# Closing stage of a decoder step: the gate's gain moved behind the transpose, idle products ahead, tile order 64-128-128, last tile stored in halves

## The reference, cut to what matters

```python
h = h + hier_moe(hn, ...)
gate = jax.nn.sigmoid(rmsnorm(h, g_ple) @ w_ple_gate)
h = h + (p @ w_ple) * gate
y = rmsnorm(h, g_final)
```

## Time and profile before

| | |
|---|---|
| time of the kernel, median of 3 | 748.12 us (746.76 to 748.71) |
| the profiled execution: its time, and its span from first to last instruction | 748.71 us, 748.7 us |
| TensorE busy | 701.7 us (94%) |
| VectorE, ScalarE, GpSimd busy | 504.4, 443.5, 143.7 us |
| mean granted clock of TensorE | 0.947 of full speed |
| HBM traffic | 322 GB/s over the span |

### The profile page before, as it was taken

The page is one execution under the profiler, slowest core; times in us unless marked ns, Lnnn a source line. Parts: engine busy times, 40 slices in busy tenths (PEclk is TensorE's granted clock), DMA queues, the critical chain, the costliest instruction groups (busy, mean ns, idle before and its releaser), DMA issues.

```text
span 748.7 us, 9169 instructions
## 1 busy us (share of the span) xinstructions
PE 701.7 (94%) x2912; PEld 470.0 (63%) x2912; DVE 504.4 (67%) x585; ACT 443.5 (59%) x436; POOL 143.7 (19%) x168
## 2 busy tenths in 40 slices
PE   2999999799999999999999999999999999994894
PEld 2646644458667777777777777777767677772441
DVE  5164013654878779787797877978779587963544
ACT  3012101344878777787777877778777777860245
POOL 4000000123302313123131221303313021311000
PEclk9899789787999999999999999999999899997797
DMA  9973031617999999999999999999999999794202
GB/s 281 371 299 113 22 113 47 249 40 313 326 423 398 426 410 408 413 400 423 398 402 427 400 415 409 402 402 395 425 408 379 402 362 428 309 346 160 55 0 70
DMA packets 30202, 233.40 MB, mean 312 GB/s; under 512 B 8023, under 2 KB 9367, under 8 KB 17375
## 3 DMA queue, kind: packets, MB, share of 16 engines
q1 hardware_dynamic: 22221, 226.96, 76.2%
q0 software_dynamic: 4480, 5.26, 2.2%
q10 hardware_dynamic: 3482, 0.94, 0.6%
HBM read 231.67 MB, written 9.32 MB: 322 GB/s over the span
## 4 chain that ended last, share of the span: by engine, by line
PE 83%; DMA 8%; DVE 5%; ACT 2%; issue 1%; POOL 1%; POOLq 0%; SPq 0%; DVEq 0%; ACTq 0%
PE ps L763 20%; PE ps L760 16%; PE ps L761 16%; PE ps L775 7%; DMA ring<-in_w_eg_dram 6%; PE ps L670 5%; PE ps L832 5%; PE ps L584 3%; PE ps L564 2%; PE ps L609 2%; PE ps L623 2%; PE ps L709 2%; PE ps L732 1%; DVE perm L1039 1%; DMA xg<-hn_rows,cur 1%
## 5 line engine op out<-in xcount | busy, mean ns | idle before, releaser
L1266 DVE TENSOR_TENSOR lo<-ring,hi 128x1536 fp32r<-128x1536 f32 x192 | 333.2, 1753 | 68.4 <-PE ps L763 51.6
L929 ACT ACTIVATE hi<-ring 128x1536 fp32r<-128x1536 f32 x192 | 280.9, 1485 | 88.8 <-PE ps L763 72.9
L760 PE MATMUL ps<-hi,xr 128*128 128x512 f32 x384 | 194.2, 506 | 0.0
L761 PE MATMUL ps<-lo,xr 128*128 128x512 f32 x384 | 152.8, 398 | 0.0
L763 PE MATMUL ps<-ring,xz 128*128 128x512 f32 x256 | 131.9, 597 | 0.0
L760 PE MATMUL ps<-hi,hr 128*128 128x512 f32 x192 | 96.2, 501 | 1.6 <-DVE hr L1278 1.6
L760 PEld LDWEIGHTS ps<-hi,xr 128*128 128x128 f32 x384 | 73.5, 191 | 36.1 <-issue 21.0
L761 PEld LDWEIGHTS ps<-lo,xr 128*128 128x128 f32 x384 | 73.4, 191 | 34.9 <-issue 23.3
L514 POOL DMA_INDIRECT moe_rows<-yo,cur x32 | 49.9, 1560 | 197.0 <-DVE yo L1256 197.0
L938 ACT ACTIVATE gu<-ps 128x512 f32<-128x512 f32 x64 | 69.3, 1082 | 30.8 <-PE ps L763 30.8
L761 PE MATMUL ps<-lo,hr 128*128 128x512 f32 x192 | 75.9, 395 | 0.0
(11 more groups left out here) (195 smaller groups left out, 591.3 us busy)
## 6 DMA issues: line engine op xcount, KB each, us to landing
ring<-in_w_eg_dram SPq DMA_DIRECT2D x32, 2048.0 KB, 14.6
ring<-in_w_eu_dram SPq DMA_DIRECT2D x32, 2048.0 KB, 15.5
ring<-in_w_ed_dram SPq DMA_DIRECT2D x31, 2048.0 KB, 16.5
ring<-in_w_in_dram SPq DMA_DIRECT2D x3, 2048.0 KB, 15.2
ring<-in_w_out_dram SPq DMA_DIRECT2D x2, 2048.0 KB, 22.3
ring<-in_w_ple_gate_dram SPq DMA_DIRECT2D x2, 2048.0 KB, 8.1
ring<-in_w_ed_dram SPq DMA_DIRECT2D x2, 1024.0 KB, 7.5
ring<-moe_rows SPq DMA_DIRECT2D x4, 512.0 KB, 5.5
```

The source lines that it names most:

```text
L760: mm(out, parts, hi[:, u % HI_RING, cut], start=begin, stop=False)
L761: done = mm(out, parts, lo[:, u % LO_RING, cut], start=False, stop=end)
L929: acti(hi[:, u % HI_RING, :], ring[:, u // 2, off:off + SPLIT], ACT.Copy).then_inc(hi_ready, counted(u, first, last))
L1266: V.tensor_tensor(lo[:, u % LO_RING, :], ring[:, u // 2, off:off + SPLIT], hi[:, u % HI_RING, :].bitcast(F32), ALU.subtract).then_inc(lo_r ...
```

## The change

The gain `g_ple` is no longer broadcast and multiplied into the rows. It is loaded once, at the start, as one value for each partition and block (`g_cols`, on ScalarE's queue), TensorE turns the rows of `h` themselves, and the copy out of PSUM multiplies by `g_cols`. Ahead of this stand 12 idle products that wait for nothing. The tiles go in the order 2, 0, 1. The adds of a tile are spread between the copies of the tile before. The last tile (tile 1) is finished and stored in two halves. The diff, cut to its core:

```diff
+LAST_ORDER = (2, 0, 1)
+        g_cols = sb("g_cols", [P, KC])
+        sig = (mixT_flat[:, 0:D], win_flat[:, 0:D], mixT_flat[:, D:2 * D])
@@ sync
-            for c, g in enumerate((g_ple, g_final.rearrange("(o d) -> o d", o=1))):
-                sp.dma_start(ring[:, 5, c * D:(c + 1) * D], g.partition_broadcast(P).rearrange(
-                    "q o d -> q (o d)")).then_inc(gl_in, 16)
+            sp.dma_start(ring[:, 5, 0:D], g_final.rearrange("(o d) -> o d", o=1).partition_broadcast(P).rearrange(
+                "q o d -> q (o d)")).then_inc(gl_in, 16)
             sp.wait_ge(y_scat, 16 * NE)
-            for t, r in enumerate(ROWS):
+            for t in LAST_ORDER:
+                r = ROWS[t]
                 for c in range(2):
                     sp.dma_start(ring[0:r, c, t * D:(t + 1) * D],
                                  moe_rows[c * NT + t * P:c * NT + t * P + r, :]).then_inc(moe_in[t][c], 16)
-            for t, r in enumerate(ROWS):
-                sp.wait_ge(y_s, t + 1)
-                sp.dma_start(y_rows[t], ple[0:r, t, :]).then_inc(out_s, 16)
+            for n, t in enumerate(LAST_ORDER[:-1]):
+                sp.wait_ge(y_s, n + 1)
+                sp.dma_start(y_rows[t], ple[0:ROWS[t], t, :]).then_inc(out_s, 16)
+            for half in range(2):
+                cut = slice(half * BLOCK, (half + 1) * BLOCK)
+                sp.wait_ge(y_s, TILES + half)
+                sp.dma_start(y_rows[LAST_ORDER[-1]][:, cut], ple[:, LAST_ORDER[-1], cut]).then_inc(out_s, 16)
@@ tensor
-            def turn_rows(t, r):
-                pe.wait_ge(nrm2, t + 1)
-                need(pe, cp2, t)
-                transposes(t, r, 6, r).then_inc(tr2, 1)
-            pe.wait_ge(gate_in, 32)
-            pe.wait_ge(moe_in[0][0], 16)
-            for _ in range(2):
-                mm(ps[:, 5, :], ident[:, :], w_ple_sb[:, 0, 0:BLOCK], start=True, stop=True)
-            turn_rows(0, P)
+            def keep_warm(n):
+                for _ in range(n):
+                    mm(ps[:, 5, :], ident[:, :], w_ple_sb[:, 0, 0:BLOCK], start=True, stop=True)
+            def turn_rows(n):
+                t = LAST_ORDER[n]
+                r = ROWS[t]
+                pe.wait_ge(h2_s, 2 * n + 2)
+                need(pe, cp2, n)
+                rows_t = h[0:r, t, :].rearrange("p (q k) -> p k q", k=KC)
+                for k in range(KC):
+                    last = tr(ps[:, 6 + k // 4, (k % 4) * P:(k % 4) * P + r], rows_t[:, k, :])
+                last.then_inc(tr2, 1)
+            keep_warm(12)
+            pe.wait_ge(gate_in, 32)
+            turn_rows(0)
...
-                        if half == 0 and t < TILES - 1:
-                            turn_rows(t + 1, ROWS[t + 1])
+                    if n < TILES - 1 and (half, k) == ((1, KC // 2 - 1) if t == TILES - 1 else (0, KC - 1)):
+                        turn_rows(n + 1)
@@ scalar
+            act.dma_start(g_cols[:, :], g_ple[0].rearrange("(q k) -> q k", k=KC)).then_inc(gc_in, 16)
...
+                if n < TILES - 1:
+...
+                else:
+                    for half in range(2):
+                        cut = slice(half * BLOCK, (half + 1) * BLOCK)
+                        if half == 1:
+                            acti(stat[0:1, 13, t:t + 1], stat[0:1, 14, t:t + 1], ACT.Sqrt)
+                        act.wait_ge(h3_s, 2 * n + half + 1)
+                        acti(ext_flat[0:r, cut], h[0:r, t, cut], ACT.Square,
+                             accum_out=stat[0:r, 8 + 4 * half, t:t + 1]).then_inc(sq2, 1)
@@ vector
-            dve.wait_ge(gl_in, 32)
...
+            def gain_turned(n):
+                t = LAST_ORDER[n]
+                r = ROWS[t]
+                dve.wait_ge(tr2, n + 1)
+                V.tensor_tensor(nT[:, :, t * P:t * P + r],
+                                ps[:, 6:8, :].rearrange("p b (k s) -> p (b k) s", s=P)[:, :, 0:r],
+                                g_cols[:, :].unsqueeze(2).to_broadcast([P, KC, r]), ALU.mult).then_inc(cp2, 1)
...
+            dve.wait_ge(gc_in, 16)
+            add_moe(0, 0)
+            add_moe(0, 1)
+            add_moe(1, 0)
+            gain_turned(0)
+            add_moe(1, 1)
+            add_moe(2, 0)
+            gain_turned(1)
+            gate_scale(0)
+            add_moe(2, 1)
+            gate_scale(1)
+            gate_scale(2)
+            gain_turned(2)
+            dve.wait_ge(gl_in, 16)
...
+                    if n == TILES - 1:
+                        dve.wait_ge(h3_s, 2 * n + half + 1)
+                        V.tensor_tensor(ple[:, t, cut], h[:, t, cut], g_last[:, cut], ALU.mult).then_inc(hg_s, 1)
...
+                else:
+                    dve.wait_ge(sq2, TILES + n + 2)
+                    link(V.tensor_tensor(stat[:, 8, t:t + 1], stat[:, 8, t:t + 1], stat[:, 12, t:t + 1], ALU.add))
+                    V.tensor_scalar(stat[:, 9, t:t + 1], stat[:, 8, t:t + 1], 1.0 / D, EPS,
+                                    ALU.mult, ALU.add).then_inc(ms2, 1)
+                    dve.wait_ge(rt2, TILES + n + 1)
+                    link(V.reciprocal(stat[:, 11, t:t + 1], stat[:, 10, t:t + 1]))
+                    dve.wait_ge(hg_s, 2)
+                    for half in range(2):
+                        cut = slice(half * BLOCK, (half + 1) * BLOCK)
+                        V.tensor_scalar(ple[:, t, cut], ple[:, t, cut], stat[:, 11, t:t + 1], None,
+                                        ALU.mult).then_inc(y_s, 1)
```

More of the change, by code:

```diff
@@ L291, in build @@
         moe_in = [[sem(f"moe_in{t}_{c}") for c in range(2)] for t in range(TILES)]
-        gate_in, gl_in = sem("gate_in"), sem("last_gains_in")
-        h2_s, sq2, ms2, rt2, nrm2 = (sem(n) for n in (
-            "moe_added", "squares2", "mean_squares2", "roots2", "rows_gained"))
+        gate_in, gl_in, gc_in = sem("gate_in"), sem("last_gain_in"), sem("gate_gain_in")
+        h2_s, sq2, ms2, rt2, hg_s = (sem(n) for n in (
+            "moe_added", "squares2", "mean_squares2", "roots2", "last_gained"))
         tr2, cp2, gt_s, sig_s, h3_s, y_s, out_s = (sem(n) for n in (
@@ L997, in _ @@
             over_pass(act, one_pass)
[L999 to L1004, removed]
+            for n, t in enumerate(LAST_ORDER):
+                r = ROWS[t]
+                act.wait_ge(h2_s, 2 * n + 2)
+                acti(junk[0:r, t, :], h[0:r, t, :], ACT.Square,
+                     accum_out=stat[0:r, 0, t:t + 1]).then_inc(sq2, 1)
+                act.wait_ge(ms2, n + 1)
+                acti(stat[0:r, 2, t:t + 1], stat[0:r, 1, t:t + 1], ACT.Sqrt).then_inc(rt2, 1)
@@ L1005, in _ @@
+            for n, t in enumerate(LAST_ORDER):
+                r = ROWS[t]
+                act.wait_ge(scale2, n + 1)
                 for half in range(2):
-                    act.wait_ge(gt_s, 2 * t + half + 1)
+                    act.wait_ge(gt_s, 2 * n + half + 1)
                     rows_t = at_half(t, half)
-                    acti(sig[:, half * BLOCK:(half + 1) * BLOCK], ps[rows_t, 2 * t + half, :], ACT.Sigmoid,
+                    acti(sig[t][0:r, half * BLOCK:(half + 1) * BLOCK], ps[rows_t, 2 * t + half, :], ACT.Sigmoid,
@@ L1016, in _ @@
+                act.wait_ge(ms2, TILES + n + 1)
                 acti(stat[0:r, 10, t:t + 1], stat[0:r, 9, t:t + 1], ACT.Sqrt).then_inc(rt2, 1)
@@ L1336, in _, with add_moe, gate_scale @@
             V.memset(spare[:, 1:2], 0.0).then_inc(experts_done, 1)
-            dve.wait_ge(gl_in, 32)
[L1340 to L1352, removed]
+            def add_moe(n, c):
+                t = LAST_ORDER[n]
+                r = ROWS[t]
+                dve.wait_ge(moe_in[t][c], 16)
+                need(dve, h2_s, 2 * n + c)
+                V.scalar_tensor_tensor(out=h[0:r, t, :], in0=ring[0:r, c, t * D:(t + 1) * D],
+                                       scalar=cw[0:r, c, t:t + 1], in1=h[0:r, t, :], op0=ALU.mult,
+                                       op1=ALU.add).then_inc(h2_s, 1)
+            def gain_turned(n):
+                t = LAST_ORDER[n]
+                r = ROWS[t]
+                dve.wait_ge(tr2, n + 1)
+                V.tensor_tensor(nT[:, :, t * P:t * P + r],
+                                ps[:, 6:8, :].rearrange("p b (k s) -> p (b k) s", s=P)[:, :, 0:r],
+                                g_cols[:, :].unsqueeze(2).to_broadcast([P, KC, r]), ALU.mult).then_inc(cp2, 1)
+            def gate_scale(n):
+                t = LAST_ORDER[n]
+                r = ROWS[t]
+                dve.wait_ge(sq2, n + 1)
+                V.tensor_scalar(stat[0:r, 1, t:t + 1], stat[0:r, 0, t:t + 1], 1.0 / D, EPS,
+                                ALU.mult, ALU.add).then_inc(ms2, 1)
+                dve.wait_ge(rt2, n + 1)
                 if t < TILES - 1:
@@ L1363, in _ @@
+            add_moe(0, 0)
[11 more added lines that the diff above has]
+            dve.wait_ge(gl_in, 16)
+            g_last = ring[:, 5, 0:D]
+            for n, t in enumerate(LAST_ORDER):
+                r = ROWS[t]
                 for half in range(2):
@@ L1364, in _ @@
```

(24 more changed lines are left out.)

21 lines of the change are left out of this document (8 added, 13 removed).

## The result

The changed kernel takes 739.93 us (median of 6, 736.94 to 742.79) against 747.74 for the kernel before beside it (743.36 to 748.71). The ratio is 0.9914 with a 95% interval of 0.9887 to 0.9941: faster by 6.4 us (4.4 to 8.4). Two later comparisons of the same two kernels gave 0.9930 and 0.9926, some 5.2 and 5.5 us. I had forecast 745.4, 2.7 us faster, and a range that ended at 742.8. The sign was right; the gain is over twice the forecast.

The account below looks back on a forecast made before the run. Bound: a chain of waits through front, block and tail. Front 1.9 us earlier, turns +2.5, clock -0.4 put TensorE's end 0.1 later; tail -2.85. Sum -2.75 from 748.12: 745.4 us, range 742.8 to 747.5.

Parts of the forecast that it names:

- the three parts: Chain split into front (to first gate product), block (gapless TensorE work) and tail (to the end), each bounded by another thing.
- the hiding: In the block, tile 2's second half (3.4 us) hides tile 0's gain copy (1.24); VectorE's adds and scales lie under products.
- the small piece's slower loads: In the front, tile 2's 64-row loads move slower: first piece lands at 690.64, second at 692.1 to 693.0.
- the turn: In front and block, strided stationary columns make eight turns cost 2.0 us; the block's two add 2.5.
- Rival 2: In front and block, the turn costs what a contiguous one does: block 2.25 shorter, front 0.4, 742.8 us; chance 0.08.
- The clock: TensorE's clock falls again near the first products and returns after 3 to 5 us: 2.0 us charged instead of 2.43.
- The rival that it holds: Around the first products the clock stays full, so all 2.0 us come back: 743.4 us; chance 0.15.
- rival 3: Turns thin TensorE's work, so the clock is half for longer or falls again: 1.7 us more, 747.1 us; chance 0.15.
- The tail: After TensorE's last product: 2.25 us saved by the half-tile finish, 0.6 by the split store, -2.85 in all.
- add_moe(1, 0): VectorE's add in the front ends by 695.6, ahead of the turn; if it ends last, a cheaper turn gains at most 0.4.

Follow-up runs that it names:

- e1: Kernel after plus six groups of eight turns behind TensorE's last product, at column steps 1, 2, 4, 8, 16 and 1: 0.114 us a turn over all steps.
- e2: Kernel after with the two idle products of before, behind the first landing of expert rows, instead of twelve: 740.05 us, ratio 0.9921.
- e6: Kernel before with twelve idle products that wait for nothing instead of its two that wait for the first landing: 745.49 us, ratio 1.0008.
- e4: Kernel after with its last tile finished and stored whole, not in halves: 740.39 us, ratio 0.9927.
- e10: Kernel after plus 72 small bf16 products behind TensorE's last: 0.026 us each with contiguous columns, 0.085 with columns 64 bytes apart.
- e7: Kernel after with first gained copy ahead of next add, 14 idle products plus one behind first turn, early square of last tile's first half: 738.57 us, again 738.40.

## Why the prediction was right or wrong

**Right: the three parts and the hiding.** The path did run through front, block and tail, `g_cols` stands nowhere in the chain, no add or scale of VectorE held a product up inside the block, and the small piece's slower loads came as priced: the second landed 1.4 us behind the first, where I had put 1.5 for a piece, and the adds were done 6.5 us after the first issue, between my ends of 6.4 and 7.3, 0.4 ahead of the value I took. The 692.1 for this piece is what the trace's 176 GB/s gives; I put the same time down to the figures of the Trainium skill ("SBUF — State Buffer", The DMA port swizzle), whose 218 GB/s give an estimate of 1.2 us a piece and 691.8. The sum went by the trace.

**Wrong: the turn.** "With the streaming half of a contiguous turn (0.054) one turn costs 0.25, eight 2.0 us" is the step that failed. Measured are 1.07 for the first turn and 1.09 and 0.89 in the block. The first turn took 0.9 us less than I charged, and the block rose by 0.4 beside its loss to the clock, not 2.5. These 3.0 us are most of the 3.8 between forecast (2.75) and the parts read (6.6); the rest is 0.4 in the adds, 0.3 in the clock and 0.4 in the tail, less 0.3 for the add that ended last. Rival 2, the turn at a contiguous one's price, is what happened, and I gave it 0.08; it would have made 5.3 us. Both rows against it were read wrongly. The earlier trace rows did show the step's price, but I scaled it by columns and added it where a turn streams beside it. The earlier trace rows was six turns in one short piece, and I divided it as if it were pace: eight contiguous turns of 120 rows right behind it, at 39.45, took 1.07 us, 0.134 each. The Trainium skill's rule that I set beside the sum ("Advanced Engine Details and Errata", SBUF Cachelines), two hits on a 16-byte line for full rate, seemed to bear the price out; e1 does not agree with it, for step 2, with two columns to a line, took 0.209 a load like step 4, and the pace was untouched by any step.

**The clock: right in kind.** It fell close to the first products, as in the forecast, for 3.4 us, a loss of 1.7 where I charged 2.0. The rival that it holds (0.15) happened in two of the eight traces with twelve idle products and a new order. That it stays low longer (rival 3) was not seen. So the idle products of this change gained nothing that e2 or e6 could measure.

**The tail: right, 0.4 short.** I had 8.3 from the last product to the end, measured 7.88: VectorE ended 5.2 behind it, not 5.6, as the squares of half a tile took 0.61 and 0.62 in the chain, not 0.75, and the two last instructions 0.88 together, not 1.08. No table load stood ahead of the square behind the sigmoid. What I did not see is that the halves themselves bring only 0.5 of the 3.3.

**The front's other terms.** add_moe(1, 0) did not end ahead of the turn, as I wrote. With a turn of 1.07 it ended last, 0.3 us behind it in the kernel after and 1.2 in e4; I had named it as what is late next. What it waits for is its load, which came 6.7 us behind the first issue in the kernel after and 7.6 in e2 and e4.

## What to carry to other kernels

A cost that is seen in the open (a longer weight load where next to nothing is streamed) must not be scaled by size and added where other work runs beside it: ask first what covers it. When tiles differ in size, the order decides what stands open at the end; a last tile whose halves finish one after the other lets the first half and its table load go under the products (2.8 of 3.3 us here). On an engine with a written order, an early step that waits for a DMA must not stand ahead of one that feeds the bound engine.

## What the runs showed of the hardware

Weight loads of 128 float32 columns took 0.14 us contiguous and 0.20 to 0.21 with a step of 2, 4, 8 or 16 elements, at the same pace of 0.114 us a turn. With 48 bf16 columns and three streamed, a load took 0.10 contiguous and 0.18 with its columns 64 bytes apart, and the pace went from 0.026 to 0.085 us a product.

With twelve or more idle products ahead of the first turn that wait for nothing, the clock of TensorE held where the pause between them and the turn was 0 or 0.4 us (e4, e10, both traces of e7), though in e4 a pause of 1.9 followed the turn. It fell in the seven traces where that pause was 1.5 to 2.4 us, with 0.3 to 1.5 behind the turn. Where it fell, half speed lasted 3.4 us, once from half a microsecond ahead of the first product. It also fell amid the experts of the kernel before, for 6.8 us from 590.9, behind 2 us in which TensorE was busy for 0.73.
